# Adding the key mask on GpSimd and the vector engine instead of with TensorE matmuls, in prompt attention A beside a merge product

## The reference, cut to what matters

```python
allowed = (s_pos[None, :] // CHUNK) <= (t_pos[:, None] // CHUNK)
score = jnp.where(allowed[None], score, NEG)
_, idx = lax.top_k(score, n_sel)                       # 256 keys per query
logits = jnp.einsum('btkgd,btjkd->btkgj', qg, k_sel) * (D_A ** -0.5)
bias = bias_a[t5_bucket(rel)]                          # by key position - query position
logits = jnp.where(valid, logits + bias, NEG)
p = jax.nn.softmax(logits, axis=-1)
o = jnp.einsum('btkgj,btjkd->btkgd', p, v_sel)
```

## Time and profile before

| | before |
|---|---|
| median of 3 runs | 3280.63 us |
| the profiled execution, its time | 3281.21 us |
| its span | 3279.4 us |
| PE busy | 3086.9 us (94%) |
| DVE busy | 1380.8 us (42%) |
| ACT busy | 954.6 us (29%) |
| POOL busy | 870.1 us (27%) |
| the 96 mask matmuls (L1737) | 229 to 390 ns each by the records, first at 2200.4, last at 2551.6 us |

### The profile page before, as it was taken

One profiled execution on the slowest core, in us unless ns is written; L12 is line 12 of the kernel. 1 busy time (PEld: TensorE's weight loads), 2 busy tenths in 40 slices (PEclk: granted clock), 3 DMA queues, 4 the chain that ended last, 5 costly groups with the idle time before them and its releaser, 6 DMA issues. The chain is left out here.

```text
span 3279.4 us, 46514 instructions
## 1 busy us (share of the span) xinstructions
PE 3086.9 (94%) x17861; PEld 2754.1 (84%) x17861; DVE 1380.8 (42%) x2323; ACT 954.6 (29%) x1951; POOL 870.1 (27%) x626
## 2 busy tenths in 40 slices
PE   5969999999999999999999999978999779899997
PEld 4969998988989989998999999867888669788875
DVE  6002564574838259700444444105555532220422
ACT  5112112122231131112333333215555331131422
POOL 1222221211212212222222222213444212143453
PEclk8989999999999999999999999989999789999998
DMA  4453322322222323333333333235432345462442
GB/s 150 83 110 85 81 64 69 81 60 71 68 69 70 82 56 88 91 96 90 100 106 104 103 107 97 73 100 167 135 106 81 93 158 188 150 226 100 150 163 103
DMA packets 385959, 342.33 MB, mean 104 GB/s; under 512 B 40040, under 2 KB 340616, under 8 KB 382264
## 3 DMA queue, kind: packets, MB, share of 16 engines
q1 hardware_dynamic: 365704, 276.32, 29.2%
q10 hardware_dynamic: 20080, 63.57, 5.8%
HBM read 252.07 MB, written 87.80 MB: 104 GB/s over the span
## 5 line engine op out<-in xcount | busy, mean ns | idle before, releaser
L627 PE MATMUL banks<-h_hi,w_in_tile_hi 128*128 128x288 f32 (+4 forms) x2608 | 590.9, 332 | 32.6 <-POOL w_in_tile_lo L510 29.5
L510 POOL TENSOR_TENSOR w_in_tile_lo<-w_in_tile_raw,w_in_tile_hi 128x512 fp32r<-128x512 f32 x228 | 297.5, 1306 | 1175.9 <-ACT w_in_tile_hi L530 1175.9
L627 PE MATMUL banks<-h_lo,w_in_tile_hi 128*128 128x288 f32 (+4 forms) x2608 | 588.6, 331 | 0.0
L627 PE MATMUL banks<-h_hi,w_in_tile_lo 128*128 128x288 f32 (+4 forms) x2608 | 587.2, 331 | 0.0
L627 PEld LDWEIGHTS banks<-h_hi,w_in_tile_hi 128*128 128x128 f32 (+1 forms) x2608 | 442.4, 188 | 68.2 <-issue 34.5
L627 PEld LDWEIGHTS banks<-h_lo,w_in_tile_hi 128*128 128x128 f32 (+1 forms) x2608 | 447.3, 188 | 35.5 <-issue 0.2
L627 PEld LDWEIGHTS banks<-h_hi,w_in_tile_lo 128*128 128x128 f32 (+1 forms) x2608 | 447.0, 188 | 35.8 <-issue 0.2
L530 ACT CAST w_in_tile_hi<-w_in_tile_raw 128x512 fp32r<-128x512 f32 x228 | 141.6, 621 | 1008.8 <-PE banks L627 919.5
L792 DVE MAX8 top<-score 128x8 f32<-128x384 f32 (+6 forms) x224 | 247.2, 1103 | 33.0 <-DVE score L795 0.9
L1220 PE MATMUL banks<-h_hi,w_in_tile_hi 128*128 128x288 f32 (+1 forms) x1056 | 234.2, 330 | 9.7 <-PEq L133 5.5
L795 DVE MATCH_REPLACE8 score<-top,score 128x384 f32<-128x384 f32 (+6 forms) x224 | 242.9, 1084 | 0.0
(11 more groups left out here) (253 smaller groups left out, 4552.6 us busy)
## 6 DMA issues: line engine op xcount, KB each, us to landing
w_in_tile_raw<-in_w_in SPq DMA_DIRECT2D x312, 256.0 KB, 2.9
w_out_tile_raw<-in_w_out SPq DMA_DIRECT2D x128, 256.0 KB, 2.5
product<-spill ACTq DMA_DIRECT2D x48, 544.0 KB, 3.4
product<-g_spill ACTq DMA_DIRECT2D x22, 544.0 KB, 2.7
g_q_raw<-product SPq DMA_DIRECT2D x68, 128.0 KB, 2.9
am_work<-product SPq DMA_DIRECT2D x16, 544.0 KB, 4.5
merged_b<-am_work ACTq DMA_DIRECT2D x16, 544.0 KB, 2.8
ma_gate_in<-product SPq DMA_DIRECT2D x16, 544.0 KB, 5.0
```

The costliest lines, as they stand in the source:

```text
L510: pool.tensor_tensor(s.w_lo[:, q, :, :], s.w_raw[:, q, :, :], s.w_hi[:, q, :, :].bitcast(F32), ALU.subtract).then_inc(lo_made, 1)
L627: last = pe.matmul(ps[0:m, 3 * slot + c, 0:w], w_[:, q, kq, 0:m], h_[:, k, t0:t0 + w], start=(k == 0 and w_ is s.w_hi and h_ is s.h_hi), s ...
```

## The change

The mask is no longer added on PE. GpSimd adds it to the near table for each unit, into a new buffer of two slots, `near_masked`; DVE takes that buffer in the place of `near`, and adds `mask` itself to the far part. The far part's instruction no longer takes a maximum along, and one maximum over the whole row takes the place of the two.

```diff
+            def mask_near(n):
+                if n < len(units):
+                    b, u = units[n]
+                    w = min(NEAR, width[b])
+                    if n in (0, H_A // 2):
+                        pool.wait_ge(table_in[1 if n else 0], 16)
+                    if u == 0 and b >= 2:
+                        pool.wait_ge(mask_in[b % 2], 16 * (b // 2))
+                    if n >= 2:
+                        pool.wait_ge(max_made, n - 1)
+                    pool.tensor_tensor(near_masked[:, n % 2, 0:w], near[:, u, NEAR - w:NEAR],
+                                       mask[:, b % 2, width[b] - w:width[b]], ALU.add).then_inc(near_ready, 1)
...
+            mask_near(0)
+            mask_near(1)
             split_lo(0)
             scale_probs(0)
+            mask_near(2)
...
             for n in range(len(units)):
                 if n + 1 < len(units):
                     scale_probs(n + 1)
+                mask_near(n + 3)
                 if n % 2 == 0:
                     split_lo(n // 2 + 2)
...
                     if n0 > c0:
-                        far_chunks += 1
-                        last = dve.tensor_scalar(prob[:, n % RING, c0:n0], ps[:, LOGITS + c % 2, 0:n0 - c0], far[:, u:u + 1],
-                                                 None, ALU.add, ALU.max, accum_out=chunk_max[:, n % RING, j:j + 1])
+                        last = dve.scalar_tensor_tensor(out=prob[:, n % RING, c0:n0], in0=ps[:, LOGITS + c % 2, 0:n0 - c0],
+                                                        scalar=far[:, u:u + 1], in1=mask[:, b % 2, c0:n0],
+                                                        op0=ALU.add, op1=ALU.add)
                     if n0 < c0 + w:
-                        t0 = n0 - (w_all - NEAR)
+                        dve.wait_ge(near_ready, n + 1)
                         last = dve.scalar_tensor_tensor(out=prob[:, n % RING, n0:c0 + w], in0=ps[:, LOGITS + c % 2, n0 - c0:w],
-                                                        scalar=far[:, u:u + 1], in1=near[:, u, t0:t0 + c0 + w - n0],
+                                                        scalar=far[:, u:u + 1],
+                                                        in1=near_masked[:, n % 2, n0 - near_at:c0 + w - near_at],
                                                         op0=ALU.add, op1=ALU.add)
                     last.then_inc(chunk_out, 1)
                 dve.wait_ge(chunk_out, first_chunk[n + 1])
-                dve.tensor_reduce(chunk_max[:, n % RING, far_chunks:far_chunks + 1], prob[:, n % RING, near_at:w_all], AX.X,
-                                  ALU.max).then_inc(near_max, 1)
-                dve.wait_ge(near_max, n + 1)
-                dve.tensor_reduce(neg_max[:, n % RING:n % RING + 1], chunk_max[:, n % RING, 0:far_chunks + 1], AX.X, ALU.max,
+                dve.tensor_reduce(neg_max[:, n % RING:n % RING + 1], prob[:, n % RING, 0:w_all], AX.X, ALU.max,
                                   negate=True).then_inc(max_made, 1)
...
                     bank = ps[:, LOGITS + c % 2, :]
-                    pe.matmul(bank[:, 0:w], s.ident_b[:, :], mask[:, b % 2, c0:c0 + w], start=True, stop=False)
                     for q_, k_ in ((q_hi, k_hi), (q_hi, k_lo), (q_lo, k_hi)):
                         last = pe.matmul(bank[:, 0:w], q_[:, u * P:(u + 1) * P], k_[:, kv, c0:c0 + w],
-                                         start=False, stop=q_ is q_lo)
+                                         start=q_ is q_hi and k_ is k_hi, stop=q_ is q_lo)
```

More of the change, by code:

```diff
@@ L1359, in attend_merge @@
         near = sb("near", [P, H_A, NEAR])
+        near_masked = sb("near_masked", [P, 2, NEAR])
         mask = sb("mask", [P, 2, SEQ], BF16)
@@ L1366, in attend_merge @@
         far = sb("far", [P, H_A])
-        chunk_max = sb("chunk_max", [P, RING, 3])
         neg_max, total, inverse = (sb(name, [P, RING]) for name in ("neg_max", "total", "inverse"))
@@ L1380, in attend_merge @@
         (v_in, far_in, k_hi_made, k_made, v_hi_made, v_made, q_in, q_hi_made, q_made,
-         logits_done, chunk_out, near_max, max_made, exp_done, inv_made, scaled, turned, pt_hi_made, pt_made, pv_done, z_in, u_made,
+         logits_done, near_ready, chunk_out, max_made, exp_done, inv_made, scaled, turned, pt_hi_made, pt_made, pv_done, z_in, u_made,
          u_stored, masks_set) = semaphores(nc, ctx, *["a_" + x for x in (
              "v_in", "far_in", "k_hi_made", "k_made", "v_hi_made", "v_made", "q_in",
-             "q_hi_made", "q_made", "logits_done", "chunk_out", "near_max", "max_made", "exp_done", "inv_made", "scaled", "turned",
+             "q_hi_made", "q_made", "logits_done", "near_ready", "chunk_out", "max_made", "exp_done", "inv_made", "scaled", "turned",
              "pt_hi_made", "pt_made", "pv_done", "z_in", "u_made", "u_stored", "masks_set")])
@@ L1430, in load_mask @@
             def load_mask(b):
-                sp.wait_ge(logits_done, first_chunk[first_of(b - 1)])
+                sp.wait_ge(max_made, first_of(b - 1))
                 sp.dma_start(mask[:, b % 2, 0:width[b]], s.masks[tokens(b), 0:width[b]]).then_inc(mask_in[b % 2], 16)
@@ L1615, in take_logits @@
                     dve.wait_ge(turned, first_bank[n - RING + 1])
-                if n in (0, H_A // 2):
-                    dve.wait_ge(table_in[1 if n else 0], 16)
-                w_all = width[units[n][0]]
+                b, w_all = units[n][0], width[units[n][0]]
                 near_at = max(0, w_all - NEAR)
-                far_chunks = 0
+                if u == 0 and b >= 2:
+                    dve.wait_ge(mask_in[b % 2], 16 * (b // 2))
                 for j, (c0, w) in enumerate(chunks(n)):
@@ L1723, in logits @@
                 kv = u // N_HEADS
-                if n == 0:
-                    pe.wait_ge(masks_set, 2)
                 if n in (0, first_of(2)):
@@ L1729, in logits @@
                     pe.wait_ge(q_made, b + 1)
-                    if b >= 2:
-                        pe.wait_ge(mask_in[b % 2], 16 * (b // 2))
                 for j, (c0, w) in enumerate(chunks(n)):
```

## The result

The changed kernel takes **3265.07 us** (median of 4 runs, 3263.11 to 3265.88) where the kernel before, on the same chip, takes 3281.83 (4 runs, 3280.07 to 3283.61): the ratio is 0.9948, with a 95% interval of 0.9936 to 0.9961. That is 16.8 us, 0.5%. Predicted were 3264.6 us and 16.0 us saved. `before` stands 1.2 us higher here than the median that the forecast started from, so the time came out nearer to the forecast (0.5 us) than the saving did (0.8 us).

What follows compares the result with a forecast made beforehand. PE was taken to bound the stage: 16.5 us of mask matmuls less 0.5 for the gate's wait gives 16.0 us, from the median 3280.63 to 3264.6 us, range 3261.5 to 3271; the other engines' additions were taken as hidden.

Steps and rivals of the forecast that it cites:

- The bound: In this stage PE is busy without gaps, 280.00 of 280 us from 2275 to 2555 us, so the stage's time is PE's.
- The sum of the mask matmuls: On PE, from the fifth unit on, the removed mask matmuls of blocks 0 to 7 are together worth 16.5 us.
- three like it leave 0.05 for the mask: 128-column groups on PE: four matmuls take 0.41 us, the last 0.12, so the mask's was taken as 0.06.
- What the gate takes back: At product(n), n = 4, 8, 12 and perhaps 16, PE waits away one mask matmul's gain each, about 0.5 us.
- The margin before the values: From the end of pt_lo to meet_values: 0.93 us falls to 0.0 to 0.2 in block 7; no wait taken.
- The 0.23: In block 7's margin: PE reaches meet_values 0.23 us earlier by the second chunk's mask matmul.
- the reads of the accumulator: On DVE behind each far part: the accumulator's read goes away, taken as 0.1 us each.
- The prices: DVE's far addition unchanged at about 0.75 us, row maximum 1.22 at 1024 elements, POOL's addition 0.85 us (0.6 at 128 columns).
- That POOL holds up DVE: Rival, chance 0.10: each POOL addition holds up DVE's chain by 0.85 us, 5.6 us back in blocks 5 to 7, 3270.2.
- That the mask matmul is nearly free: Rival, chance 0.06: each mask matmul on PE costs only 0.04 us, so 3.7 us are won, 3276.9.
- the sustained 131 ns at 512 columns: Skill rule for PE's matmul spacing: all 96 mask matmuls worth an estimated 11 us, time about 3270.
- The slower rival: Rival, chance 0.02: POOL's additions bind from 3.0 us each, the kernel is slower from 3.4; at 3.6, 3299 us.

Runs made afterwards that it cites:

- PE's part alone: The kernel before without its 96 mask matmuls on PE, the mask added nowhere in this stage: 3264.57 us, ratio to before 0.9946.
- additions alone: The changed kernel with 96 matmuls of the old widths on a tile of zeros back on PE: 3282.12 us, ratio to before 1.0.

## Why the prediction was right

**The bound.** Read rightly: PE had no gaps, and what was taken from it came off the time. The two halves of the change show it apart: without the mask matmuls 3264.6, with only the additions 3282.1. The additions were put at nothing for PE; the traces show 0.4 to 0.65 us for them.

**The sum of the mask matmuls.** Between the second `meet_values` and the end the logits became 16.7 us shorter, and from the fifth unit on, as the working counts, 17.1 where it had 16.5. By block, from block 1 on: 0.99, 1.36, 1.78, 2.78, 2.86, 3.11 and 3.59 us, where the working had 0.96, 1.40, 1.84, 2.32, 2.80, 3.24 and 3.68. One term is off, the matmul on 128 columns: taken as 0.06, measured as 0.12 to 0.13 in blocks 0 and 4, which is 0.8 us too little in these two blocks. The widths of 384 and 512 were taken slightly too high, 0.3 us in all, and the unforeseen cost of the additions works the same way, so a part of the good agreement is luck. The step that failed is "three like it leave 0.05 for the mask". In the earlier trace rows the group was 0.41 us and the last f32 matmul 0.12, but the three without the mask take 0.28 and not 0.36:

```profile
2244.25 0.23 PE L1748 MATMUL banks<-am_k_hi,am_q_hi 128*128 128x128 f32 x1
2244.31 0.27 PE L1748 MATMUL banks<-am_k_lo,am_q_hi 128*128 128x128 f32 x1
2244.42 0.27 PE L1748 MATMUL banks<-am_k_hi,am_q_lo 128*128 128x128 f32 x1
2244.53 0.30 PE L1760 MATMUL banks<-ident,am_prob 128*128 128x128 f32 x1
```

The first one holds PE up for 0.06 us, since its weights are loaded beside the 512 columns in front of it (the records of the weight loads start at 2244.01 here); with the mask in front they were loaded at 2244.42 only, and the lead was lost. That the lead is the cause was read from the two traces and not tried by itself; that the price is 0.12 to 0.13 in front of any width was tried.

**What the gate takes back.** Foreseen as 0.5 us at n = 4, 8, 12 and 16. Measured from turn to product: 0.13, 0.13, 0.13 and 0.18 more, 0.57 in all, and nothing from 20 on. At product(8), against the earlier trace rows:

```profile
2256.56 0.53 PE L1729 MATMUL banks<-am_u_hi,w_br_b_tile_hi 128*128 128x288 f32 x2 [0.58 <-DVE am_work L1682]
```

**The margin before the values.** Foreseen: 0.0 to 0.2 us in block 7 and no wait, 0.4 to 0.8 in blocks 4 to 6. Measured: 0.28 to 0.32, and 0.78, 0.66 and 0.40. The sum came out near, but two of its terms were wrong, and they nearly cancel. The 0.23 was subtracted because PE reaches `meet_values` earlier by the second chunk's mask. But that mask matmul stands ahead of the logits for which DVE's second far part waits as well, so it makes both earlier. And the reads of the accumulator, taken as 0.1 us each, cost next to nothing. The second far parts before, with PE's part alone, and in the changed kernel:

```profile
2524.28 0.48 DVE L1627 TENSOR_SCALAR_CACHE_REDUCE am_prob<-banks,am_far 128x256 f32<-128x256 f32 x1
2510.51 0.48 DVE L1627 TENSOR_SCALAR_CACHE_REDUCE am_prob<-banks,am_far 128x256 f32<-128x256 f32 x1
2509.73 0.47 DVE L1642 SCALAR_TENSOR_TENSOR am_prob<-banks,am_far,am_mask 128x256 f32<-128x256 f32 x1
```

| us, at meet_values(28) in block 7 | before | PE's part alone | additions alone | changed |
|---|---|---|---|---|
| last logits matmul of the unit to `meet_values` (starts) | 4.09 | 4.07 | 4.09 | 4.07 |
| last logits matmul to DVE's second far part (starts) | 0.43 | 0.51 | 0.44 | 0.48 |
| second far part to `pt_lo` (starts) | 1.45 | 1.45 | 2.05 | 2.04 |
| `pt_lo` | 1.28 | 1.28 | 1.28 | 1.28 |
| margin (what is left, to 0.01) | 0.93 | 0.84 | 0.33 | 0.28 |

From PE's last logits matmul to `meet_values` next to nothing changes (0.02 us). The additions lengthen DVE's chain from the second far part on by 0.58 to 0.60 us, all of it the maximum (1.13 us from its start to `pt_lo`, where the two maxima took 0.53). Of the rest, 0.05 to 0.08 us come from the first far part: DVE gets from the first to the second in 0.67 us at best (2509.06 to 2509.73, and 0.68 with the read of the accumulator and without the mask matmul). Four matmuls in 0.92 us left it a wait between the two (0.83 from the first to the second); three in 0.69 leave none, so the second far part starts a little later after its logits. From the first far part to `pt_lo` the growth is 0.42 us, and not the 0.5 to 0.7 foreseen, because that wait has gone out of it.

**The prices.** The far addition with a bf16 mask takes 750 ns on 512 columns, its f32 like took 749. The maximum over 1024 takes 1220 ns, as foreseen. POOL's addition takes 677 ns on 256 columns and 426 on 128, where 0.85 and 0.6 were taken.

**The rivals.** That POOL holds up DVE did not happen: none of DVE's steps in the chain became longer, and its near part waited for `near_masked` once, 2.0 us at unit 0, where the stage waits for its loads. Only `q_lo`, which reads two tensors in SBUF, went from a mean of 1221 to 1281 ns: the four of eight that start while an addition of POOL is running with 0.2 us or more left take 1.32 to 1.37 us, the others 1.21 to 1.23. With the addition done twice it shows in both directions:

```profile
2312.47 0.68 POOL L1514 TENSOR_TENSOR am_spare_near<-am_near,am_mask 128x256 f32<-128x256 f32 x1
2312.90 1.32 DVE L1622 SCALAR_TENSOR_TENSOR am_q_lo<-am_q_raw,am_q_hi 128x1024 fp32r<-128x1024 f32 x1
2313.10 1.66 POOL L1516 TENSOR_TENSOR am_near_masked<-am_near,am_mask 128x256 f32<-128x256 f32 x1
```

The first addition delays `q_lo` by 0.10 us, and the second, started while `q_lo` runs, takes 1.66 us and not 0.68. The Trainium skill, "SBUF — State Buffer", two separate sides, has an exclusive lock, held for the whole instruction, between GpSimd and vector instructions with two SBUF inputs. The traces agree: `q_lo` and POOL's addition wait for each other, and the instructions with one operand from PSUM kept their length. That the mask matmul is nearly free is refuted by both halves of the change. Its neighbour, the sustained 131 ns at 512 columns of "TensorE: Matmul & The Clock Gate", Back-to-back issue gap, in the Trainium skill, didn't hold for this stream either: three f32 matmuls stand 0.23 us apart, and the bf16 one was worth 0.22. The slower rival had its mechanism right: at 3.4 us a unit POOL made the kernel slower than before. Its point was put too high: by the stage's sum PE is passed at 3.0 us, by the blocks with short periods the loss began below 2.7 us.

**Where the trace can mislead.** From the first logits to the second `meet_values` the traces of kernels that do the same work there differ: 39.3 us before, 38.9 in both traces of the changed kernel, 40.0 and 37.1 in the two halves. The longest has the lowest granted clock between 2220 and 2240 us (0.69) and the shortest the highest (0.80); this is a mean over stretches at the 1.2 and at the 2.4 GHz level, and PE waits there for loads and splits. Differences of 2 us in this start-up between single traces are no effect of an edit. The dense part is another matter: there three traces of the same work agree within 0.04 us.

## What to carry to other kernels

Where the bound engine's records touch for hundreds of microseconds, price a removed instruction by the distance from start to start, together with its neighbours. Then look at each place where the bound engine nearly waits. An instruction removed between the end of what starts the awaited work and the wait itself gains nothing, for the wait grows by as much; the others count in full. If it stands ahead of that point, it moves both the awaited work and the wait, and the margin between them stays.

An engine that is busy for two thirds of a stage may have 0.3 us of room. Its room is the margin at the place where the bound engine takes its result, and an addition to its chain is nearly free up to that. Weigh a helper engine's load against the bound engine's by the shortest repeating period, not by the sum over the stage.

## What the runs showed of the hardware

A bf16 matmul on 128 columns in front of f32 matmuls costs TensorE 0.12 to 0.13 us at the full clock, as much as one on 256 columns (0.12), and one on 512 costs 0.22 to 0.23. GpSimd adds an f32 and a bf16 tensor of 128 partitions by 256 in 0.68 us, and of 128 by 128 in 0.43. On the vector engine a bf16 operand in SBUF beside an operand in PSUM made no difference (750 against 749 ns on 512 columns), and the read of the accumulator behind an instruction (83 ns by its record) cost at most 0.02 us of the chain. A vector instruction with two SBUF operands and a GpSimd addition waited for each other: 1.22 us became 1.32 to 1.37, and 0.68 became 1.66.
